# A hybrid decoder layer on one core: tile 1's first projection is moved ahead of tile 0's sixth, and the first weight chunk is loaded and summed in two halves

## The reference, cut to what matters

```python
def hybrid_layer(x, mem, ...):                 # x: 1 x 4096 x 1024, mem: 1 x 256 x 1024
    h = rmsnorm(x, norm_g)
    proj = h @ w_in                            # 1024 x 3072: six groups of 512 columns
    sb_q, sb_k, sb_v, sb_gate, lru_x, lru_gate, xa_q, xa_gate = split(proj)
    sb_out = stick_breaking_attention(rmsnorm(q), rmsnorm(k), v)      # 8 heads of 64
    lru_out = rg_lru(causal_depthwise_conv(lru_x), ...)               # 256 channels
    mk, mv = split(rmsnorm(mem, mem_g) @ w_mem_kv)
    xa_out = softmax_attention(rmsnorm(xq), rmsnorm(mk), mv)          # 4 heads of 64
    y = concat(sb_out * silu(sb_gate), lru_out * silu(lru_gate), xa_out * silu(xa_gate))
    return x + y @ w_out                       # 1024 x 1024
```

## Time and profile before

| | |
|---|---|
| median of 3 runs | 1509.79 us (1508.33 to 1510.03) |
| the profiled execution's own time | 1510.54 us |
| its span, first to last instruction | 1508.9 us |
| mean granted TensorE clock | 0.998 |
| PE busy | 1478.1 us (98%) |
| DVE busy | 1049.5 us (70%) |
| ACT busy | 932.2 us (62%) |

### The profile page before, as it was taken

One profiled execution on the slowest core, in us unless ns is written; L12 is line 12 of the kernel. 1 busy time (PEld: TensorE's weight loads), 2 busy tenths in 40 slices (PEclk: granted clock), 3 DMA queues, 4 the chain that ended last, 5 costly groups with the idle time before them and its releaser, 6 DMA issues.

```text
span 1508.9 us, 31170 instructions
## 1 busy us (share of the span) xinstructions
PE 1478.1 (98%) x11412; PEld 719.2 (48%) x11412; DVE 1049.5 (70%) x1923; ACT 932.2 (62%) x1724; POOL 305.0 (20%) x303
## 2 busy tenths in 40 slices
PE   4999999999999999999999999999999999999998
PEld 2454444444444444444444444444444444444443
DVE  7989766667666667666667666667666676666685
ACT  7988655577555576555576555576555576555573
POOL 3132111222111222111222111222111222111220
PEclk9999999999999999999999999999999999999999
DMA  9556655665554665554665554654554654555755
GB/s 397 192 125 127 137 136 110 147 134 118 123 133 107 149 132 117 126 129 109 152 129 118 129 127 109 153 125 119 132 125 112 153 125 115 136 122 115 154 113 134
DMA packets 466697, 205.44 MB, mean 136 GB/s; under 512 B 439712, under 2 KB 439904, under 8 KB 465504
## 3 DMA queue, kind: packets, MB, share of 16 engines
q1 hardware_dynamic: 466512, 204.77, 58.2%
q10 hardware_dynamic: 144, 0.13, 0.0%
HBM read 55.46 MB, written 50.46 MB: 70 GB/s over the span
## 4 chain that ended last, share of the span: by engine, by line
PE 90%; DVE 5%; ACT 2%; DMA 1%; issue 1%; DVEq 0%; ACTq 0%; SPq 0%
PE bank L2022 27%; PE bank L2024 27%; PE bank L2023 27%; PE bank L2233 2%; PE bank L2069 2%; PE bank L2093 1%; DVE w_pair L1348 1%; PE bank L2111 1%; PE bank L2120 1%; DMA wo_pair<-in_w_out 1%; PE bank L2164 1%; PE bank L2159 0%; PE bank L2161 0%; PE bank L2160 0%; DVE fail_and_take L1594 0%
## 5 line engine op out<-in xcount | busy, mean ns | idle before, releaser
L2022 PE MATMUL bank<-w_pair,x_hi 128*128 128x512 f16 x1520 | 577.5, 380 | 5.2 <-DVE w_pair L1348 4.5
L2023 PE MATMUL bank<-w_pair,x_hi 128*128 128x512 f16 x1520 | 576.7, 379 | 0.0
L2024 PE MATMUL bank<-w_pair,x_lo 128*128 128x512 f16 x1520 | 576.6, 379 | 0.0
L1073 ACT ACTIVATE qk_raw<-bank,unscale 128x512 f32<-128x512 f32 x32 | 22.0, 687 | 426.9 <-PE bank L2024 424.1
L2022 PEld LDWEIGHTS bank<-w_pair,x_hi 128*128 128x128 f16 x1520 | 148.6, 98 | 182.9 <-issue 9.6
L2024 PEld LDWEIGHTS bank<-w_pair,x_lo 128*128 128x128 f16 x1520 | 148.9, 98 | 179.9 <-issue 0.8
L2023 PEld LDWEIGHTS bank<-w_pair,x_hi 128*128 128x128 f16 x1520 | 148.9, 98 | 168.3 <-issue 1.5
L2022 PE MATMUL bank<-wo_pair,y_hi 128*128 128x512 f16 x480 | 181.9, 379 | 0.0
L2023 PE MATMUL bank<-wo_pair,y_hi 128*128 128x512 f16 x480 | 181.9, 379 | 0.0
L2024 PE MATMUL bank<-wo_pair,y_lo 128*128 128x512 f16 x480 | 181.9, 379 | 0.0
L808 POOL TENSOR_TENSOR fail_and_take<-fail_and_take,seen 128x512 f32<-128x512 f32 x32 | 41.2, 1286 | 675.1 <-ACT fail_and_take L969 675.1
(11 more groups left out here) (296 smaller groups left out, 2429.6 us busy)
## 6 DMA issues: line engine op xcount, KB each, us to landing
xy<-in_x SPq DMA_DIRECT2D x32, 512.0 KB, 3.8
spare<-in_x SPq DMA_DIRECT2D x30, 512.0 KB, 4.0
out<-spare SPq DMA_DIRECT2D x29, 512.0 KB, 2.6
gate_kept<-gate SPq DMA_DIRECT2D x32, 256.0 KB, 2.3
v_kept<-v_sb SPq DMA_DIRECT2D x32, 256.0 KB, 2.1
fail_and_take<-v_sb SPq DMA_DIRECT2D x64, 128.0 KB, 2.3
q_kept<-heads_t SPq DMA_DIRECT2D x32, 256.0 KB, 4.0
k_kept<-heads_t SPq DMA_DIRECT2D x32, 256.0 KB, 4.2
```

Source lines behind the costliest of these rows:

```text
L2022: pe.matmul(dst, hi[:, k, :], pair[:, 0, k, :], start=k == 0, stop=False)
L2023: pe.matmul(dst, hi[:, k, :], pair[:, 1, k, :], start=False, stop=False)
L2024: last = pe.matmul(dst, lo[:, k, :], pair[:, 0, k, :], start=False, stop=k == KD - 1)
```

## The change

Tile 1's `project(0)` is taken out of step 1 and done in step 0 between `project(4)` and `project(5)` of tile 0, by a new function `second_first`. For this tile 1 gets row buffers of its own, `y_hi` and `y_lo` (`rows_in`), and its first two projections get banks of their own, `HEADS` and `SMALL` (`proj_bank`). What lay in `y_hi` and `y_lo` (`mk_raw`, `mk_squares`) goes to `turned[:, 1]` and `v_sb[:, 1]`. ACT and DVE get a new order at the end of step 0: `rows_high` before `chunk_high(5)`, without the wait for `proj_done[5]`; `chunk_factor(5)` before `chunk_low(4)`; `rows_low` before `chunk_low(5)`; `heads_high` and `memory_values(1)` before the high half of v; `values_low` behind the heads' low halves. Beside it, the first weight chunk comes in two transfers of 1 MB, and ACT sums its halves apart, with one more small DVE operation that joins the sums.

```diff
-        mk_raw = y_hi[:, :, :].rearrange("p k t -> p (k t)").bitcast(F32)
-        mk_squares = y_lo[:, :, :].rearrange("p k t -> p (k t)").bitcast(F32)
+        mk_raw = turned[:, 1, :, :].rearrange("p c t -> p (c t)").bitcast(F32)
+        mk_squares = v_sb[:, 1, :, :].rearrange("p a n -> p (a n)").bitcast(F32)
...
+        FIRST_BANKS = (HEADS, SMALL)
+
+        def rows_in(tile):
+            return (y_hi, y_lo) if isinstance(tile, int) and tile == 1 else (x_hi, x_lo)
+
+        def proj_bank(tile, c):
+            return FIRST_BANKS[c] if isinstance(tile, int) and tile == 1 and c < 2 else PROJ[c % 2]
...
-            load_chunk(0)
+            front = slice(0, KD // 2)
+            sp.dma_start(stage[0][:, front, :], w_in_g[ORDER[0]][:, front, :]).then_inc(front_loaded, 16)
+            back = slice(KD // 2, KD)
+            sp.dma_start(stage[0][:, back, :], w_in_g[ORDER[0]][:, back, :]).then_inc(stage_loaded[0], 16)
...
+            def first_sum():
+
+                for waited, ks, at in ((front_loaded, slice(KT, KD // 2), 1), (stage_loaded[0], slice(KD // 2, KD), 0)):
+                    act.wait_ge(waited, 16)
+                    flat = slice((ks.start - KT) * GC, (ks.stop - KT) * GC)
+                    last = act.activation(sum_waste[:, flat], stage[0][:, ks, :].rearrange("p k n -> p (k n)"), ACT.Abs,
+                                          accum_out=row_max[:, at, KT:KT + 1])
+                last.then_inc(w_sum, 1)
...
                     if spreads(n + 1):
                         have(act, s["x_scaled"], n + 1)
-                        if A:
+                        if early:
+                            have(act, proj_done[5], n - 1)
+                        elif A and not first:
                             have(act, proj_done[5], n)
-                        act.activation(x_hi[:, :, :], x_t32[:, :, :], ACT.Copy).then_inc(s["x_hi_done"], 1)
+                        act.activation(rows_in(n + 1)[0][:, :, :], x_t32[:, :, :], ACT.Copy).then_inc(s["x_hi_done"], 1)
...
                 if first:
+                    rows_high()
                     chunk_high(5)
...
                 if first:
                     memory_values(0)
                     out_sum(6, (0,))
-                    rows_high()
+                    heads_high()
+                    memory_values(1)
...
                 if first:
-                    heads_high()
-                    memory_values(1)
                     out_sum(6, (1, 2))
...
+                if c == 0:
+                    w_next(dve.tensor_tensor(rows[:, KT:KT + 1], rows[:, KT:KT + 1], row_max[:, 1, KT:KT + 1], ALU.max))
...
                 if first:
+                    chunk_factor(5)
                     chunk_low(4)
-                    chunk_factor(5)
                     w_next(dve.tensor_scalar(taps, taps, unscale[:, G_LRU:G_LRU + 1], 1.0 / VDOWN, ALU.mult, ALU.mult))
                     silu_lru()
+                    rows_low()
                     chunk_low(5)
                     silu_stick()
...
-                if first:
-                    rows_low()
-                    values_low()
...
                 if first:
+                    values_low()
                     memory_keys()
                     memory_values_top()
                     memory_keys_norm()
...
+                def second_first():
+
+                    have(pe, s["x_hi_done"], 1)
+                    pe.wait_ge(w_factor, CH - 2)
+                    for k in range(KD):
+                        for part in range(2):
+                            pe.matmul(FIRST_BANKS[0][:, :], y_hi[:, k, :], w_pair[:, ORDER[0], part, k, :],
+                                      start=k + part == 0, stop=False)
+                    have(pe, s["x_lo_done"], 1)
+                    for k in range(KD):
+                        last = pe.matmul(FIRST_BANKS[0][:, :], y_lo[:, k, :], w_pair[:, ORDER[0], 0, k, :],
+                                         start=False, stop=k == KD - 1)
+                    last.then_inc(proj_done[0], 1)
...
-                project(0, [(s["gate_sb"], n - 1), (s["out0_read"], n - 3)])
+                if not early:
+                    project(0, [(s["gate_sb"], n - 1), (s["out0_read"], n - 3)])
...
-                project(1, [(s["v_read"], n - 1), (s["out_ready"], n - 3)])
+                project(1, [] if early else [(s["v_read"], n - 1), (s["out_ready"], n - 3)])
...
                 project(4, [(s["gate_x"], n)])
+                if static and n == 0:
+                    second_first()
```

More of the change, by code:

```diff
@@ L306, in hybrid_layer @@
         w_step = sem("w_step")
+        front_loaded = sem("front_loaded")
         lam_made = sem("lam_made")
@@ L1072, in body @@
                         have_dma(act, stored, 0)
-                    act.activation(q_raw[:, :, :], PROJ[0][:, :].rearrange("p (h d) -> p h d", d=HD), ACT.Copy,
+                    act.activation(q_raw[:, :, :], proj_bank(n, 0)[:, :].rearrange("p (h d) -> p h d", d=HD), ACT.Copy,
                                    scale=unscale[:, G_Q:G_Q + 1])
-                    act.activation(squares, PROJ[0][:, :], ACT.Square, scale=unscale[:, G_Q:G_Q + 1]
+                    act.activation(squares, proj_bank(n, 0)[:, :], ACT.Square, scale=unscale[:, G_Q:G_Q + 1]
                                    ).then_inc(s["q_read"], 1)
@@ L1095, in body @@
                     have(act, s["q_sum"], n)
-                    act.activation(k_raw[:, :, :], PROJ[1][:, :].rearrange("p (h d) -> p h d", d=HD), ACT.Copy,
+                    act.activation(k_raw[:, :, :], proj_bank(n, 1)[:, :].rearrange("p (h d) -> p h d", d=HD), ACT.Copy,
                                    scale=unscale[:, G_K:G_K + 1])
-                    act.activation(squares, PROJ[1][:, :], ACT.Square, scale=unscale[:, G_K:G_K + 1]
+                    act.activation(squares, proj_bank(n, 1)[:, :], ACT.Square, scale=unscale[:, G_K:G_K + 1]
                                    ).then_inc(s["k_read"], 1)
@@ L1308, in chunk_top @@
                     w_next(dve.tensor_reduce(g_rows[:, KT:KT + 1], g_in[:, KT:], AX.X, ALU.max, apply_absolute_value=True))
-                dve.wait_ge(stage_loaded[st], 16 * STAGE[:c + 1].count(st))
+                if c:
+                    dve.wait_ge(stage_loaded[st], 16 * STAGE[:c + 1].count(st))
+                else:
+                    dve.wait_ge(front_loaded, 16)
                 w_next(dve.tensor_reduce(row_max[:, c % 2, 0:KT], stage[st][:, 0:KT, :], AX.X, ALU.max,
@@ L1698, in rows_low @@
                     if spreads(n + 1):
-                        dve.tensor_tensor(x_lo[:, :, :], x_t32[:, :, :], x_hi[:, :, :], ALU.subtract
+                        high, low = rows_in(n + 1)
+                        dve.tensor_tensor(low[:, :, :], x_t32[:, :, :], high[:, :, :], ALU.subtract
                                           ).then_inc(s["x_lo_done"], 1)
@@ L2038, in project @@
                         have(pe, signal, tile)
-                    if static and n in (1, 2) and c == 0:
+                    if static and n == 2 and c == 0:
                         for k in range(KD):
@@ L2052, in project @@
                             pe.wait_ge(w_lo, highs(c) - KD + k + 1)
-                        pair_product(PROJ[c % 2][:, :], x_hi, x_lo, w_pair[:, ORDER[c]], proj_done[c], [k])
+                        pair_product(proj_bank(n, c)[:, :], *rows_in(n), w_pair[:, ORDER[c]], proj_done[c], [k])
                 last_one, after, end = near_end(n)
@@ L2169, in body @@
                     chunk_wide(0)
-                if A:
+                early = static and n == 1
+                if A and not early:
                     if spreads(n):
@@ L2181, in body @@
                     chunk_wide(2)
-                early = static and n == 1
                 third = static and n == 2
@@ L2203, in body @@
                     memory_product(0, 1)
+                if early:
+                    have(pe, s["gate_sb"], n - 1)
                 project(2, [(s["q_read"], n)])
@@ L2211, in body @@
                     out_wide()
+                if early:
+                    have(pe, s["v_read"], n - 1)
                 project(3, [(s["k_read"], n)])
```

2 lines of the change are left out of this document (1 added, 1 removed).

## The result

The changed kernel is slower, by more than was forecast. In 16 runs of each in turn the median went from 1508.97 us (1506.13 to 1510.03) to 1512.70 us (1509.81 to 1515.08), a ratio of 1.0027 [1.0020, 1.0033]. The profiled execution took 1512.18 us with a span of 1510.4 us.

A forecast was written before the change was run, and what follows sets the result against it. PE bounds the steady loop, so earlier gains or losses pass through one for one. -1.05 (shorter way) + 1.69 (clock) + 0 (front) = +0.65 on 1509.79 gives 1510.4 us; own range 1509.4 to 1511.6, wider range 1507.2 to 1512.6.

The forecast's parts named there:

- rival 5: The moved projection itself waits because x_hi or w_factor is late; 3.5 us in hand at 67.0; chance 0.02.
- rival 4: Hole before values_wide closes, v and memory_keys being quicker than summed: 1505.6 us, or 1508.3 with DVE as bound; chance 0.09.
- Rival 3: New wait on w_out before values_wide, its late landing added in full to the hole; 1511.4 at +1 us; chance 0.07.
- the chain through v: From project(5)'s end through v's halves, memory_keys and memory_values_top to values_wide: PE stands 3.2 us.
- the clock term: Low clock behind the hole, paid by project(1): 1.69 us as in the earlier trace, bounds 0 and 5.19.
- rival 1: The hole before values_wide doesn't bring the clock down, leaving only -1.05 us: 1508.7 us; chance 0.22.
- rival 2: Low clock lasts through project(1), deciding from over 4.1 us lost: 1513.9 us at the bound, 1512 halfway; chance 0.10.
- The gain of 1.05 us for the shorter way: PE reaches values_wide at 80.6 instead of 81.65 us, as no projection separates it from project(5): -1.05 us.
- The front: First chunk in two halves: first projection 0.15 to 0.3 us earlier, PE's time from 36.5 us unchanged: 0.

The follow-up runs named there:

- the reordered kernel: Changed kernel with memory_values(1) and heads_high before out_sum(6), and DVE's memory_keys and memory_values_top before the heads' low halves: mean 1508.88 us, ratio 1.0002.
- the changed kernel twice: The changed kernel profiled first, then run once more unchanged beside the partly filled ones: the repeat had mean 1512.46 us, ratio 1.0024.
- three filled ones: Changed kernel with 4, 8 or 15 extra matmuls in the hole behind project(5): means 1508.79, 1509.58 and 1508.68 us.
- the move alone: Changed kernel with the first chunk's single load and sum put back, so only the projection is moved: mean 1512.21 us, ratio 1.0022.
- the two transfers with one sum: Kernel before with the first chunk loaded by two transfers on its old semaphore and summed at once: mean 1508.83 us, ratio 1.0001.
- the filled kernel before: Kernel before with 12 extra matmuls in the hole behind tile 0's project(5): mean 1507.45 us, ratio 0.9992.
- the front alone: Kernel before with only the first chunk in two transfers, two sums and a joining DVE operation: mean 1509.94 us, ratio 1.0007.

## Why the prediction was wrong

**Right: the schedule.** The moved projection began at 66.64 (67 forecast), `y_hi` was written from 62.14 (62.4), `w_out` landed at 72.86 (72.7), `project(5)` ended at 77.16 (77.4), the heads' low halves at 78.0 (77.9), the hole was 3.33 us (3.2), released by DVE's diagonal, and the broadcast began at 80.49 (80.6). No wait on `x_hi` or `w_factor` took over, so rival 5 fell, and rival 4 fell with the hole of 3.33 us. In the reordered kernel, which closes this hole, 2.45 us of waiting appear at `near_scores`.

Rival 3 is there in small. In the six profiles that keep the changed kernel's order (the changed kernel twice, three filled ones, the move alone) the diagonal is ready 7.58 to 7.59 us after ACT begins the sum of `w_out`; counted from the end of `project(5)` it is 3.28 us in the changed kernel's first profile and 3.55 in its second. So the landing of `w_out`, and what stands behind it on ACT and DVE, set the hole's end, 0.1 to 0.35 us later than the 3.2 us summed in the prediction for the chain through v. It made the second hole 3.60 us.

**Wrong: the size of the clock term.** The step is "I take the same 1.69". It fails in two ways.

First, after. The first profiled execution lost 2.96 us there, and with this number the sum closes: the broadcast came 1.16 us earlier (1.05 forecast), -1.16 + 2.96 = 1.80, and the joint lies 1.81 us later. In the mean execution, filling the hole took 3.5 to 3.9 us off, and 1.1 us off the kernel before. So the term rose by 2.4 to 2.8 us, and was forecast as 1.69 in both. The argument against rival 1, that the hole is longer, was the right one, and it should have been carried on to the size. This is rival 2's mechanism at a lower price than its point of 4.1 us.

How much of it is the clock? The granted clock gives a bound: 2 x (1 - clock) x span is the time at the lower level, 7.7 us in the mean of the 16 runs (0.9974) and 7.1 in the later 11, and PE loses half of that at most, 3.9 and 3.6 us (each execution's clock is given to a thousandth, 1.5 us of such time). In before it is 2.1 to 2.8 us (0.9993 to 0.9991), at most 1.0 to 1.4 lost. A part of this time costs nothing, because it lies in the hole or behind PE's last matmul. In the two profiles of the changed kernel 2.96 of 7.5 us and 1.5 of 4.4 us were lost; by these shares, an estimate, the mean execution loses 2.4 to 3.0 us. About 1 us of what the fill gave is thus not covered by the clock, and its cause stays open (the last section has a candidate). Nor does a mean clock under 1.000 show a fall behind the hole. In the profile of the two transfers with one sum the clock stayed up behind a hole of 2.72 us, and the mean is 0.999 all the same, from the end, where PE is done:

```profile
1505.00:1506.00 1.00, 0.00 (x0) 0.00 (x0) 0.00 (x0) 0.00 (x0) 0.00 (x0) 0.50 0.09 25
1506.00:1507.00 1.00, 0.00 (x0) 0.00 (x0) 0.00 (x0) 0.00 (x0) 0.00 (x0) 0.50 0.04 12
```

Such time at the end was between 0 and 3.2 us in the 14 profiles.

Second, before. The 1.69 us of the earlier trace rows were taken as what the kernel pays each time. It doesn't: 35 of its 99 executions read a granted clock of 1.000, which leaves room for 0.75 us at most. And not all of it was there to have: the filled kernel before shows the broadcast at 80.33, behind DVE's diagonal, so of the 1.69 only 1.2 us reach `project(1)`. The gain of 1.05 us for the shorter way holds against the profiled execution and not against one whose clock stayed up: filled against filled the broadcast begins at 80.33 and 80.40, so the move had nothing to win there.

The Trainium skill ("TensorE: Matmul & The Clock Gate", section "What's actually happening") says that the place of the transition varies from run to run. The profiles agree: the clock fell 1.2 us behind the restart in before, and in the changed kernel 1.0 and 0.6 us ahead of it, inside the hole. Whether it falls varies as well. It fell with holes of 2.45 us (reordered), 2.55 (before), 3.33 and 3.60 (changed, twice) and 3.35 (the move alone), and it did not with 2.70 (four matmuls), 2.72 (two transfers, one sum) and 3.23 us (the front alone). The low stretch lasted 3.4 to 3.5 us in four of these five and 6.8 us in the first profile of the changed kernel. I used that rule for rival 1 alone, where it bore on the baseline as well.

**Wrong: nothing outside the span.** The time outside the span rose by 0.35 us (1.54 to 1.89). The two transfers alone have 1.72, the move alone 1.71: each seems to bring about half. Which instructions or buffers make it was not settled.

**The front** was forecast at 0. It seems to start the first projection 0.48 us earlier (17.92 against 18.40 us), but the 18.40 is the latest of the 14 profiles: without the front it starts at 17.88 to 18.40, with it at 17.76 to 18.21. The wait of DVE for ACT's sum is gone in all profiles with the front (0.18 to 0.33 us without); no more than that is shown, and at the memory's weights (35.90 to 36.73 us with it, 35.95 to 37.88 without) nothing of it can be seen. Alone it cost 1.0 us of span in one group, with the hole filled 0.4, and in the changed kernel about 0.2: it gains nothing, and how much it costs stays open. Its hole of 3.23 us and more time at the lower clock in the mean (0.9986, 4.1 us) fit the same mechanism, though its own profile shows no fall. The hole was longer because `w_out` took 8.5 us there instead of 7.8, and `x_hi` stands behind it on ACT; that this transfer is slower because of the front isn't shown, since it took 7.6 to 8.5 us over all profiles.

**The sum.** In means the change costs 4.0 us against the 16 runs of before beside it, 3.6 in the later group. Of the 4.0, 2.8 are the difference of what the two holes cost beyond their length by the fills (3.9 and 1.1), most of it the clock; the filled kernels differ by the other 1.2, and time outside is 0.25 of those (1.80 to 1.55). The last 0.98 us, in the mean spans of the two filled kernels, has no place in their profiles (joints at 142.38 and 142.44) and is near what one group can tell. The forecast's base was off as well: the three runs shown had a median of 1509.79, the next 13 brought it to 1508.97. Against the later base the change cost 3.7 us where 0.65 was forecast; from the base used, 1512.7 lies just above the range.

## What to carry to other kernels

A hole on PE has two prices: its length, and the clock behind it. The second isn't proportional: in the changed kernel 2.7 us cost little over none and 3.3 to 3.6 us cost 3.5 to 3.9 us more, while 2.55 us in the kernel before cost 1.1. So a change that merges two small slacks into one longer hole should be priced by the clock first. Fill such a hole with matmuls to learn what it costs before moving work across it, and take the price of a clock event from many executions, not from the one that was profiled.

## What the runs showed of the hardware that had not been expected

**The rate at the start varies most.** The first projection starts at 17.8 to 18.4 us and issues every 0.427 us until the rate doubles, at a place that was anywhere from 20.4 to 23.9 us in 14 profiles. Two kernels whose program up to there is the same, with four and with eight added matmuls, timelines of PE:

```profile
20.41 0.49 PE L2049 MATMUL bank<-w_pair,x_hi 128*128 128x512 f16 x1
20.73 0.38 PE L2050 MATMUL bank<-w_pair,x_hi 128*128 128x512 f16 x1
```

```profile
23.17 0.59 PE L2049 MATMUL bank<-w_pair,x_hi 128*128 128x512 f16 x1
23.59 0.38 PE L2050 MATMUL bank<-w_pair,x_hi 128*128 128x512 f16 x1
```

The granted clock of the windows reads 1.00 all the while, so this loss is seen in the spacing only. In the six profiles that keep the order of before or of the changed kernel and in which the hole was under 3 us and the clock stayed up behind it, a rise at 22.6 us or earlier left the joint near 142.4 us (142.37 to 142.44), one at 23.1 gave 143.14 and one at 23.6 gave 144.02: in these, a late rise goes with up to 1.6 us. The profile with eight added matmuls is the last of them; whether its other executions rose late too, and read higher for that, their times don't show.

**What is left varies by one store.** From the joint (145.41 in the rows above) to DVE's last instruction it takes 1360.24 to 1360.35 us in all 14 profiles. What follows, the last store of `out`, took 2.7 to 5.0 us until the end of the span: 5.0 before, 4.7 after, 2.7 and 2.8 in their filled kernels, 3.5 in the changed kernel's second profile. The two profiled executions thus differ by 1.5 us in their spans and by 1.81 at the joint. The store took less than 3 us in five of the six profiles whose joint lies before 142.5 us, and 3.4 to 5.0 us in seven of the eight with a later joint. Whether a late joint lengthens the store, so that the 1 us of the fills that the clock doesn't cover comes from it, stays open.
